# Input projection by blocks of tokens, with the tiles of x prepared between the column blocks, and the casts of the expert weights issued at the start

## The reference

```python
h = rmsnorm(x, g_mix)                       # x: (4, 4096, 1024) f32
proj = h @ w_in                             # 1024 x 2304: qa, ka, va (512 each), qb (512), kb, vb (128 each)
oa = dilated_attention(qa, ka, va)          # 8 heads, windows/dilations (128,1) (512,4) (2048,16)
ob = windowed_gqa_sink(qb, kb, vb, sink)    # 8 q heads, 2 kv heads, +-128
x = x + concat(rmsnorm(oa), rmsnorm(ob)) @ w_out
x = x + hier_moe(rmsnorm(x))                # 32 experts, top 1 of 4 groups, top 2 of 8 in it
x = x + (p @ w_ple_proj) * sigmoid(rmsnorm(x) @ w_ple_gate)
y = rmsnorm(x)
```

## Time and profile before

| | |
|---|---|
| median of 3 runs | 1676.73 us (1671.33, 1676.73, 1725.31) |
| the profiled execution | 1667.38 us |
| its span on the slowest core (core 6) | 1666.1 us |
| spans of the 8 cores | 1635.5 to 1666.1 us |
| TensorE busy with matmuls | 1117.0 us (67%) |
| VectorE, ScalarE, GpSimd busy | 572.1, 474.3, 259.4 us |
| chain that ended last | TensorE 45%, DMA 29%, VectorE 9%, issue 9% |
| q0 (GpSimd's DMAs), share of 16 engines | 64.7% of the span |
| q1 (SyncE's DMAs) | 20.7% of the span |
| HBM read and written | 350.94 and 113.79 MB |

### The profile page before, as it was taken

How to read it: one execution, slowest core, us unless ns; L and a number is a source line. 1 busy time by engine, 2 the same in 40 slices (tenths; PEclk the granted TensorE clock), 3 DMA queues, 4 the chain that set the end, 5 groups by cost and what they waited for, 6 DMA issues and landing times.

```text
span 1666.1 us, 22293 instructions; the slowest of 8 cores (1635.5 to 1666.1 us)
## 1 busy us (share of the span) xinstructions
PE 1117.0 (67%) x7796; PEld 704.6 (42%) x7835; DVE 572.1 (34%) x1050; ACT 474.3 (28%) x756; POOL 259.4 (16%) x285
## 2 busy tenths in 40 slices
PE   0126999999999885664645185766767657731784
PEld 0123444556656443433434174545645446520332
DVE  4452221445545434444414321111212112110476
ACT  1231111434323554322213021111212112212764
POOL 2010330000001002000000121223322223237300
PEclk9999999978768797877766597878878878875887
DMA  4749699999999999999998489789898797799813
GB/s 80 177 134 127 84 113 111 110 111 109 112 110 109 110 122 128 146 183 130 150 129 131 151 256 270 201 229 242 230 287 211 211 271 192 184 168 203 174 77 127
DMA packets 79267, 266.50 MB, mean 160 GB/s; under 512 B 17033, under 2 KB 23209, under 8 KB 69936
## 3 DMA queue, kind: packets, MB, share of 16 engines
q0 software_dynamic: 53680, 153.65, 64.7%
q1 hardware_dynamic: 25472, 111.36, 20.7%
HBM read 350.94 MB, written 113.79 MB: 279 GB/s over the span
## 4 chain that ended last, share of the span: by engine, by line
PE 45%; DMA 29%; DVE 9%; issue 9%; ACT 5%; POOL 2%; DVEq 0%; SPq 0%; another core or an unknown queue 0%; ACTq 0%; POOLq 0%
DMA arena<-h2d,arena 17%; PE ps L460 10%; PE ps L561 6%; DMA arena<-xl 6%; PE ps L1164 5%; PE ps L543 4%; DMA ohd<-arena 4%; PE ps L1145 4%; PE ps L531 4%; PE ps L1361 3%; PE ps L601 2%; PE ps L877 1%; PE ps L1124 1%; POOL arena L1312 1%; PE ps L435 1%
## 5 line engine op out<-in xcount | busy, mean ns | idle before, releaser
L547 ACT ACTIVATE arena<-ps 128x1024 bf16<-128x1024 f32 (+4 forms) x152 | 137.3, 916 | 192.6 <-PE ps L543 192.3
L1145 PE MATMUL ps<-arena 128*128 128x192 bf16 x2048 | 176.2, 247 | 1.1 <-ACT arena L1131 1.1
L1145 PEld LDWEIGHTS ps<-arena 128*128 128x128 bf16 x2048 | 171.5, 98 | 8.1 <-issue 1.3
L1164 PE MATMUL ps<-arena 128*96 128x512 bf16 x512 | 153.9, 459 | 15.2 <-DVE arena L1152 11.7
L460 PE MATMUL ps<-arena 128*128 128x512 bf16 (+1 forms) x744 | 161.2, 377 | 1.0 <-issue 0.2
L1124 PE MATMUL ps<-arena 96*128 96x96 bf16 x512 | 40.7, 245 | 159.8 <-DMA arena<-h2d,arena 159.8
L877 PE MATMUL ps<-arena 128*128 128x512 bf16 x242 | 74.9, 471 | 87.1 <-DVE arena L858 42.4
L1177 POOL DMA_INDIRECT y<-arena x64 | 60.6, 946 | 368.6 <-ACT arena L1169 289.7
L561 PE MATMUL ps<-arena 128*65 128x128 bf16 (+5 forms) x784 | 112.2, 266 | 0.8 <-ACT arena L547 0.8
L460 PEld LDWEIGHTS ps<-arena 128*128 128x128 bf16 x760 | 74.0, 99 | 88.3 <-issue 2.7
L1164 PEld LDWEIGHTS ps<-arena 128*96 128x96 bf16 x512 | 71.8, 150 | 85.8 <-issue 66.7
(11 more groups left out here) (161 smaller groups left out, 1426.1 us busy)
## 6 DMA issues: line engine op xcount, KB each, us to landing
wbf<-wexp POOLq DMA_DIRECT2D x72, 1024.0 KB, 169.2
arena<-wbf SPq DMA_DIRECT2D x72, 1024.0 KB, 16.4
arena<-wexp POOLq DMA_DIRECT2D x24, 1024.0 KB, 80.4
arena<-xl SPq DMA_DIRECT2D x40, 512.0 KB, 8.9
y<-arena SPq DMA_DIRECT2D x16, 512.0 KB, 2.7
arena<-w_in POOLq DMA_DIRECT2D x3, 1536.0 KB, 18.8
h2d<-arena SPq DMA_DIRECT2D x16, 256.0 KB, 17.2
arena<-w_out POOLq DMA_DIRECT2D x1, 2048.0 KB, 108.5
```

The source lines that it names most:

```text
L547: S.op("act", lambda e: e.activation(out=PT[pi][0:nk, :, 0:w], in_=ps[0:nk, sb:sb + 2, 0:w], func=AF.Exp, scale=0.125), reads=[b_ps[sb], b ...
L1145: self.T.op("pe", lambda e, k=k, f=f, bk=bk, wt=wt, c0=c0: e.matmul(psb(bk)[:, c0:c0 + CAP], lhsT=wt[sl][:, k, 128 * f:128 * (f + 1)], rhs ...
L1164: self.T.op("pe", lambda e, f=f, j=j, hf=hf, bk=bk: e.matmul(psb(bk)[0:HC, :], lhsT=hid[s][:, f, HC * j:HC * (j + 1)], rhs=wd_b[sl][:, f, ...
```

## The change

Six things change.

- The gains are loaded into buffers of their own and no longer wait for each other. The loads of w_rg, w_re, the biases and `sink`, and the Exp of `sink`, stand behind the loads of the first four tiles of x.
- There are three weight buffers and four for x. The buffers of x, of the normalised tile and of the tables' intermediate values lie in the space of Q, K and V of group B.
- GpSimd's queue issues first the two weight blocks of group A, then `wkb` (four loads that don't wait for each other), then the third block, then at once the casts of the first 16 experts.
- A tile of x is prepared in three steps, each in another call of `x_step`: square, sum and root (`x_sq`); reciprocal and scaling (`x_front`), behind which the buffer's next load is issued; transposition and gain (`x_back`). The order in one call is `x_back` of tile i-2, `x_front` of i-1, `x_sq` of i. The factor 1/1024 moves into the square.
- The projection of group A runs over blocks of 512 tokens: for each block all its column blocks. Six calls of `x_step` stand ahead of block 0, and one ahead of every third group in it (of more in block 4). Group B follows, also by blocks of tokens.
- The tables are computed between the groups of A and those of B.

```diff
-        for i, (g, nk) in enumerate(((g_mix, 8), (g_ffn, 8), (g_ple, 8))):
-            S.dma("sp", ..., writes=[b_gall])
...
+        for i, (g, r0, nk) in enumerate(((g_mix, 0, 8), (g_ffn, 8, 8), (g_ple, 16, 8), (g_grp_a, 24, 4), (g_grp_b, 28, 4))):
+            S.dma("sp", ..., reads=[b_gall], writes=[b_gd[i]])
...
-        xs = [A.alloc((1024,), F32) for _ in range(2)]
-        wblk = [A.alloc((8, 768), BF16) for _ in range(2)]
+        wblk = [A.alloc((8, 768), BF16) for _ in range(3)]
+        A.top = r2_off
+        NXS = 4
+        xs = [A.alloc((1024,), F32) for _ in range(NXS)]
+        tmpf = A.alloc((1536,), F32)
+        xn = [A.alloc((1024,), BF16) for _ in range(2)]
...
         load_wblk(0)
         load_wblk(1)
+        (four loads of wkb)
+        load_wblk(2)
+        for ei in list(b_cast)[:16]:
+            cast_expert(ei)
...
+        def x_step():
+            i = xc[0]
+            xc[0] += 1
+            for f_, lag_ in ((x_back, 2), (x_front, 1), (x_sq, 0)):
+                if 0 <= i - lag_ < 24:
+                    f_(i - lag_)
+
+        for t in range(NXS):
+            x_load(t)
+        (loads of w_rg, w_re, b_rg, b_re, sink on SyncE's queue)
+        S.op("act", lambda e: e.activation(out=esink, in_=esink, func=AF.Exp), reads=[b_esink], writes=[b_esink])
+        for _ in range(6):
+            x_step()
+        for tb in range(6):
+            cols = [(0, w0, 128 * j, QT_A[:, j, :], b_QA) for j in range(4)] if tb < 4 else []
+            cols += [(0, w0, 512 + 128 * j, KT_A[:, j, :], b_KA) for j in range(2)]
+            cols += [(1, w1, 128 * j, KT_A[:, 2 + j, :], b_KA) for j in range(2)]
+            cols += [(1, w1, 256 + 128 * j, VT_A[:, j, :], b_VA) for j in range(4)]
+            for ci, (wi, w, c0, dst, db) in enumerate(cols):
+                if ci % 3 == 2 or (tb == 4 and ci % 2):
+                    x_step()
+                proj_fm(b_wblk[wi], lambda k, w=w, c0=c0: w[:, k, c0:c0 + 128], dst, db, [(512 * tb, 512)])
+        tables()
+        for tb in range(5):
+            blk = [(512 * tb, 512 if tb < 4 else 128)]
+            for j in range(4 if tb < 4 else 0):
+                proj_fm(b_wblk[2], ..., QT_B[:, j, :], b_QB, blk)
+            for g in range(2):
+                proj_fm(b_wkb, ..., KT_B[:, g, :], b_KB, blk)
+            proj_fm(b_wblk[2], ..., VT_B, b_VB, blk)
-        for ei in list(b_cast)[:2]:
-            cast_expert(ei, [b_hT[4]])
-        load_wblk(2)
-        for ei in list(b_cast)[2:16]:
-            cast_expert(ei)
```

More of the change, by code:

```diff
@@ L313, in build_nc @@
         S.op("pool", lambda e: e.memset(gall, 0.0), writes=[b_gall])
-        for i, (g, nk) in enumerate(((g_mix, 8), (g_ffn, 8), (g_ple, 8))):
[L315 to L332, removed]
+        b_gd = [Buf("gd%d" % i) for i in range(5)]
+        for i, (g, r0, nk) in enumerate(((g_mix, 0, 8), (g_ffn, 8, 8), (g_ple, 16, 8), (g_grp_a, 24, 4), (g_grp_b, 28, 4))):
+            S.dma("sp", lambda e, g=g, r0=r0, nk=nk: e.dma_start(out=gall[r0:r0 + nk, :],
+                                                                 in_=g.rearrange("(k p) -> k p", p=128)),
+                  reads=[b_gall], writes=[b_gd[i]])
         S.op("pe", lambda e: e.transpose(out=psb(0)[:, 0:32], in_=gall[0:32, :], identity=ident_f[0:32, 0:32]),
-             reads=[b_gall, b_ident], writes=[b_ps[0]])
+             reads=[b_gall, b_ident] + b_gd, writes=[b_ps[0]])
         S.op("dve", lambda e: e.tensor_copy(out=gT, in_=psb(0)[:, 0:32]), reads=[b_ps[0]], writes=[b_gT])
@@ L366, in build_nc @@
         b_QA, b_KA, b_VA, b_QB, b_KB, b_VB = [Buf(n) for n in ("QA", "KA", "VA", "QB", "KB", "VB")]
[L368 to L384, removed]
@@ L385, in build_nc @@
         hT = A.alloc((8, NLOC), BF16)
-        xs = [A.alloc((1024,), F32) for _ in range(2)]
-        xn = [A.alloc((1024,), BF16) for _ in range(2)]
-        wblk = [A.alloc((8, 768), BF16) for _ in range(2)]
+        wblk = [A.alloc((8, 768), BF16) for _ in range(3)]
         st1 = A.alloc((24, 4), F32)
         wkb = A.alloc((8, 2, 128), BF16)
[L391 to L397, removed]
+        keep = A.top
@@ L398, in build_nc @@
+        A.top = r2_off
[3 more added lines that the diff above has]
+        xn = [A.alloc((1024,), BF16) for _ in range(2)]
+        assert A.top <= r3_off
+        A.top = keep
+        b_tmpf = Buf("tmpf")
+        b_wkb = [Buf("wkb%d" % i) for i in range(4)]
         b_hT = [Buf("hT%d" % i) for i in range(6)]
-        b_xs = [Buf("xs%d" % i) for i in range(2)]
+        b_xs = [Buf("xs%d" % i) for i in range(NXS)]
         b_xn = [Buf("xn%d" % i) for i in range(2)]
-        b_wblk = [Buf("wblk%d" % i) for i in range(2)]
+        b_wblk = [Buf("wblk%d" % i) for i in range(3)]
@@ L405, in load_wblk @@
             S.dma("pool", lambda e, bi=bi: e.dma_start(
-                out=wblk[bi % 2], in_=w_in[:, 768 * bi:768 * (bi + 1)].rearrange("(k p) c -> p k c", p=128)),
-                writes=[b_wblk[bi % 2]])
+                out=wblk[bi], in_=w_in[:, 768 * bi:768 * (bi + 1)].rearrange("(k p) c -> p k c", p=128)),
+                writes=[b_wblk[bi]])
         b_cast = {ei: Buf("cast%d" % ei) for ei in range(1, NEXP) if ei == 1 or ei % 4 != 1}
@@ L419, in build_nc @@
         load_wblk(1)
-        gmb = gT[:, 0:8].unsqueeze(2).to_broadcast([128, 8, 128])
[L422 to L432, removed]
+        for g_ in range(2):
+            for hh_ in range(2):
+                S.dma("pool", lambda e, g_=g_, hh_=hh_: e.dma_start(
+                    out=wkb[:, :, g_, 64 * hh_:64 * hh_ + 64],
+                    in_=w_in[:, 2048 + 64 * g_:2048 + 64 * g_ + 64].rearrange("(k p) c -> p k c", p=128)),
+                    writes=[b_wkb[2 * g_ + hh_]])
@@ new lines, in x_front @@
+        def x_front(t):
+            s, b = t % NXS, t % 2
+            S.op("dve", lambda e: e.reciprocal(out=st1[:, t, 2:3], in_=st1[:, t, 1:2]),
+                 reads=[b_st1[t]], writes=[b_st1[t]])
+            S.op("dve", lambda e: e.tensor_scalar(out=xn[b], in0=xs[s], scalar1=st1[:, t, 2:3],
+                                                  scalar2=None, op0=ALU.mult),
+                 reads=[b_xs[s], b_st1[t]], writes=[b_xn[b]])
+            if t + NXS < 24:
+                x_load(t + NXS)
@@ L433, in build_nc, with x_back @@
+        def x_back(t):
             pb = t % 2
             for k in range(8):
[L435 to L439, removed]
+                S.op("pe", lambda e, k=k: e.transpose(out=psb16(pb)[:, 128 * k:128 * (k + 1)],
+                                                      in_=xn[pb][:, 128 * k:128 * (k + 1)], identity=ident_b),
+                     reads=[b_xn[pb], b_ident], writes=[b_ps[pb]])
+            S.op("dve", lambda e: e.tensor_tensor(
@@ new lines, in build_nc @@
+        w0, w1, w2 = wblk
+        xc = [0]
+        def x_step():
[6 more added lines that the diff above has]
+            x_load(t)
+        S.dma("sp", lambda e: e.dma_start(out=wr[:, :, 0:4], in_=w_rg.rearrange("(k p) g -> p k g", p=128)),
+              writes=[b_wr])
+        S.dma("sp", lambda e: e.dma_start(out=wr[:, :, 4:36], in_=w_re.rearrange("(k p) g -> p k g", p=128)),
+              writes=[b_wr])
@@ new lines, in build_nc @@
+        S.dma("sp", lambda e: e.dma_start(out=rbias[:, 0:4], in_=b_rg.partition_broadcast(128)),
+              writes=[b_rbias])
+        S.dma("sp", lambda e: e.dma_start(out=rbias[:, 4:36], in_=b_re.partition_broadcast(128)),
+              writes=[b_rbias])
+        S.dma("sp", lambda e: e.dma_start(out=esink, in_=sink.partition_broadcast(128)),
+              writes=[b_esink])
+        S.op("act", lambda e: e.activation(out=esink, in_=esink, func=AF.Exp), reads=[b_esink], writes=[b_esink])
```

51 lines of the change are left out of this document (33 added, 18 removed).

## The result

The changed kernel takes **1687.3 us** (median of 20 runs; before, beside it, 1675.7 us in 20 runs). The ratio is **1.0071**, 95% interval 1.0047 to 1.0096: slower by 12 us, where 1618 us was forecast.

What follows compares the result with a forecast made beforehand. TensorE bounds the projection but is hardly used in the first 142 us; DMA comes second. 61 + 161 + 16 + 11 + 4 = 253 against 304; 51 + 4 - 2 = 53 off 1667.4 gives 1614, forecast 1618, range 1588 to 1655.

Steps and rivals of the forecast that it cites:

- Start: Before the projection: sink lands at 45 us, first projection matmul at 61 us, bounds 46 and 68.
- The upper bound of 52: At the start: sink lands by 52 us at most, from four x tiles landing at 43 plus 9.
- Rival 4: Projection: x served one tile at a time, ScalarE's square waits 14.4 us per tile; 1753 us in all, chance 0.07.
- Matmuls and tiles between the columns: Projection: 744 matmuls stay at 161 us; 20 tiles' transposes among them add 16 us, bounds 9 and 20.
- Loads of x: Projection: x paced at 6.7 us per tile under the casts, costing 11 us over 18 steps, bounds 0 and 50.
- Whole packets (rival 3): Projection: x waits for 17 cast descriptors each turn, 10.9 us per tile, 76 lost, 1690 us in all; chance 0.04.
- Tables: Behind the first 64 projection groups: VectorE's work on the tables costs 4 us, bounds 0 and 14.
- Weights and casts: GpSimd's queue from the start: costed at nothing; all casts end about 61 us earlier, the last near 850.
- Afterwards: Attention loses up to 3 us by the clock; output projection gains about 4; experts load and gather as before.
- The sum: To the end of projection: 253 us against 304, 51 earlier; with what follows, 53 us gained.
- rival 1: Start and projection: first matmul at 46 to 50, x at 6.1 us per tile; about 1592 us in all, chance 0.15.

Runs made afterwards that it cites:

- e3: Changed kernel with the casts of the first 16 experts issued behind the tables instead of right behind the weights; ratio to before 1.0343.
- e12: Changed kernel with own buffer names for w_re and b_re, so the five small loads are issued without waits between; ratio to before 0.9853.
- e4: e2 with the casts of the first 16 experts also moved behind the tables; ratio to before 1.0088.
- e5: e2 with six buffers for x instead of four; ratio to before 0.9609.
- e2: Changed kernel with sink's load and Exp ahead of x's first tile, w_rg, w_re and biases behind its last; 1601.9 us, ratio to before 0.9608.
- e11: Changed kernel with only w_rg and w_re loaded behind the last tile of x; ratio to before 0.9757.
- e9: e2 without interleaving: all 24 tiles of x prepared ahead of the first projection group, casts beside them; ratio to before 0.9879.
- e10: e5 with 14 instead of 16 experts' casts at the start and 5 instead of 3 behind w_out's load; ratio to before 0.9612.

## Why the prediction was wrong, point by point

- **Start: the step that failed.** It put the sink's landing at 45 us and the first projection matmul at 61. They came at 109 and 131 (core 4). It had seen that every Square waits for the last small load, and that small packets take turns. It let the small ones take turns with w_in only, and for the chain of five loads, with its waits, it took over the 9.0 us that the chain needs alone. But w_rg needed 30 us beside w_in, so w_re was not issued before 39.2 and ran beside the casts (46 us instead of 19 in e3), and b_re and the sink followed one by one, each after a landing. Without the waits (e12) the sink lands at 45.9; that this is the value assumed is chance, since the sum reached it by another way. The upper bound of 52 was built from x and the 9.0 us of the small loads alone; it left out the very packets that the sentence named, so the range held no such case.
- **Nothing had a rival for it.** Rival 4 had the right waiting engine, ScalarE's Square, but the wrong load: x, not the sink. And the second way, SyncE's queue with the fifth tile of x behind the small loads, was not named, although the text says what is queued in which order.
- **Matmuls and tiles between the columns: right.** From the first projection matmul to attention the prediction has 161 + 16 + 4 = 181 us without the waits for x. The three kernels in which TensorE hardly waits for x take 182 (e3), 183 (e4) and 184 (e5). The transpositions alone were put too high: 160 of them, for 20 tiles, are busy 12.2 us, 16 was assumed.
- **Loads of x: the pace right, the price too low.** They land after 19.8 / 21.6 / 22.8 us (least, median, most) from 140 to 260 us, near 20 foreseen, and the squares of tiles 5 to 23 come 6.85 us apart, 6.7 foreseen. But the whole stretch takes 212 us, 29 more than without waits, where 11 were foreseen; in e2, where more tiles are read beside w_in, 197. On core 4 TensorE is idle for 28.9 of the 210 us from 131 on, 5.35 of them at the tables. And part of the price goes with the clock: the granted clock is 0.93 from 150 to 250 us, that is, part of the time is at 1.2 GHz, and L452's matmuls are busy 174.3 us (161.2 before, 169.6 in e4), while in e4, with next to no waits for x, 38 to 144 us are at 1.00. The prediction left this out; how the 29 us divide between waits and clock the runs don't show.
- **Whole packets (rival 3).** What speaks against it is the pace of 6.85 us per tile, where it has 10.9. The Trainium skill, "DMA: Bandwidth & Descriptors", section "Queues, rings and completion order", has turns of whole packets of 9 to 17 descriptors; counts as even as 2131 and 2130 don't tell how long a turn is, and no run here shows it.
- **Tables: right.** TensorE waits 5.35 us in one gap, 4 foreseen.

```profile
297.98 41.73 PE L452 MATMUL ps<-arena 128*128 128x512 bf16 x196 [5.35 <-DVE arena L443]
```

- **Weights and casts: half right.** Costed at nothing on GpSimd, which holds; but the transfers had a victim at the start. The last cast was foreseen near 850; in e2 the DMA share falls from 1.00 after 840. In the changed kernel, with attention late, the DMA engines ran dry (a share of 0.15 from 650 to 700 us), since the next casts are issued only at attention's end, at 699; a share of 0.95 or more up to the last cast was foreseen.
- **Afterwards: right in kind.** Attention took 372 us (368 before, in the medians). The output projection took 260 instead of 273 us in the median, with fewer casts beside it (a DMA share of 0.76 on core 4, before 0.91). So 30 us lost at attention's start are 21 at the experts' and 12 at the end.
- **The sum.** In the medians attention starts 83 us later than the 253 foreseen: 63 by the start (124 instead of 61), 20 by the stretch behind it. With the start mended the sum comes out near: e11 starts its matmuls at 56, attention at 262 and the experts at 904, where 61, 254 and 895 were foreseen, and its ratio of 0.9757 is a gain of some 40 us, 53 foreseen. e2 moves only the small loads and comes out 62 us under its neighbour at 1664.2; that this is near 53 is in part luck, since its matmuls start 25 us sooner than foreseen. In rival 1 the sum gives 1594, not 1592.

Half settled: why, once the casts run, w_rg and w_re take 53 to 61 us to land in e2, e5, e9 and e11 and 46 in the changed kernel. 64 packets per DMA engine at the casts' 0.55 us make 35. In e2 w_rg is issued at 129.6 behind loads of x in the same queue, the last of which is squared at 151.4; from there to its landing at 189.4 are 38 us. w_re has no such load ahead of it, and its last packets come late there too; that stays open.

## What to carry to other kernels

When a transfer is moved behind others, price it in packets, beside what the other queues will be doing at the moment at which it is then issued, and follow its waits: here 2048 packets of 16 and 128 bytes, with the biases and the sink behind them, took 9 us alone and 100 us beside weight loads and casts. Look for every engine that stands in line behind it, the issuing queue too; one tiny operation placed ahead of a long row (the Exp of eight numbers) makes the whole row wait. And a front stage that gets faster keeps its gain only until the next thing that the same DMA queue must deliver: w_out in e4, the last casts in e10.

## What the runs showed of the hardware

- Beside casts two queues take turns packet by packet: 2131 and 2130 packets in 100 us with 3.9 and 3.6 KB each, 837 and 838 in 30 us with 3.8 KB and 16 bytes. It is no rule for every mix: beside the small packets of wkb (0.2 KB each) q0 passes ten for one of x, as e9 shows from 45 to 52 us:

```profile
q0 software_dynamic: 2348, 0.51, 88.9%
q1 hardware_dynamic: 231, 0.83, 38.3%
```

- The x queue gets 77 GB/s beside casts (7.74 MB in 100 us) and 150 beside w_in and wkb (4.51 MB in e9 from 30 to 60 us).
- Issuing on SyncE's queue can itself take long: in e12, behind w_rg with no wait in between, issuing w_re took 11.48 us and b_rg 11.41, where 0.4 us is usual.
- Short waits of TensorE in dense work go with a lower clock: the granted clock of 131 to 341 us is 0.94, against 1.00 in the projection before and in e4 from 38 to 144 us, neither of which has such waits.
